# Moving ScalarE's request for a filter piece's rows from the end of an odd expert pair to the middle of the next even pair

## The chip, the cores and the metric

One NeuronCore of a Trainium2 chip runs the whole program. The metric is the device time of one execution in microseconds, lower is better. Times of the kernel before are the median of three runs; the trace is of one further, profiled execution.

## What is computed

One step of a two-layer network over 384 tokens of width 1024 (128 context tokens, 256 latent tokens). Layer 0 mixes tokens by attention, layer 1 by a long convolution whose filters are themselves computed. After each mixer comes a mixture of experts. The parts that matter here are the experts and the filters:

```python
# experts: 32, two chosen per token, hidden width 256
a = einsum('nd,edh->neh', t, w_gate); b = einsum('nd,edh->neh', t, w_up)
act = silu(a) * b * combine[:, :, None]
out = einsum('neh,ehd->nd', act, w_down)
# filters of layer 1: they depend on no token
filt = hdn @ w3 + b3
filt = filt * exp(-t_norm * exp(log_decay))
norm = sum(abs(filt), ...)          # and the spectrum of filt by a DFT
```

Everything is float32.

## The kernel before, in words

The experts are worked off in 16 **pairs** (q = 0 to 15), the same loop in both layers. A pair has up to 64 token rows per expert. TensorE multiplies the gathered tokens with the gate and up weights (line 903, 32 matmuls), ScalarE takes the silu out of the accumulator (line 1311), VectorE multiplies with the up half (line 1768), TensorE turns the result (line 909) and multiplies it with the down weights (line 917, 16 matmuls); ScalarE and VectorE copy one half each of the output (lines 1321 and 1785), and GpSimd scatters it to memory. In the midst of pair q TensorE also turns the gathered tokens of pair q + 1 (line 886) and ScalarE copies half of them out (line 1287, `gathered`). SyncE requests the weights: those of gate and up when line 903 of two pairs earlier is done (line 422), those of down likewise after line 917 (line 427). One pair's weights are 6 MB, in two ring slots.

A pair with more rows than fit has an **extra round**, which stands ahead of the pair proper: `extra(q)`, a conditional on every engine. There TensorE turns eight blocks (line 933), ScalarE and VectorE copy four each (lines 1297 and 1732), and TensorE's line 903 waits for both copies. In layer 0 pairs 6 and 7 have such a round in the trace.

The filters of layer 1 are computed in eight **pieces** (f = 0 to 7) inside layer 0's expert loop, in time that the engines have left. One piece takes three pairs:

- `load_filter` requests six transfers: two halves of the decay rows (line 414, 128 KB each, broadcast over all partitions), and for each half the rows of `w3` (line 416, 64 KB) and of `b3` (line 417, 1 KB). Its two waits are for TensorE's third tap matmul and ScalarE's decays of the piece before, since the tiles `eld` and `w3c` are single.
- `decay(f)` on ScalarE at the end of even pair 2f waits for both decay rows, then takes one exponential in place (line 1157), three more (line 1164), with a table load ahead (line 1157), and one back to silu (line 1166).
- In odd pair 2f + 1 TensorE makes the taps (line 608), VectorE multiplies them with the decays (line 1455), and ScalarE takes their absolute values (`sizes`, line 1170) at the pair's end.
- In even pair 2f + 2 TensorE makes the spectra (lines 625 to 630) and the sizes (line 639), ScalarE and VectorE copy them (lines 1176 and 1470), and ScalarE requests their store (`store_spectra`, line 1182, 768 KB) behind the next `decay`.

Each engine works its instructions off in the order of the program. On ScalarE that order holds for its transfer requests too: a request stands behind the waits ahead of it, and what follows a request waits until it is issued. The first piece is requested by SyncE, the other seven by ScalarE.

Of the kernel before, what the change touches and what calls it, by code (L numbers as in the profile page):

```python
# [149 lines left out]
def build(nc, a):  # L150

    ctx = ExitStack()
    with ctx:
# [5 lines left out]
        def sem(name):  # L159
            if name not in sems:  # L160
                sems[name] = ctx.enter_context(nc.semaphore(name))
            return sems[name]
# [141 lines left out]
        def turn_bank(q, half):  # L304
            return bank[half + (6 if q == 0 else 0)]
# [101 lines left out]
        def load_filter(sp, f):  # L407
            if f >= 1:
                sp.wait_ge(sem("taps_mm"), 3 * f)
                sp.wait_ge(sem("dec_set"), 4 * f)  # L410
            o, n = FILT[f]
            for d in range(2):
                lo = (2 * o + d) * D + n * FC
                sp.dma_start(eld[:, d * FC:(d + 1) * FC], a["hy_log_decay"][0, lo:lo + FC].partition_broadcast(P))\
                    .then_inc(sem("decay_in"), 16)
                sp.dma_start(w3c[0:FH, d * FC:(d + 1) * FC], a["hy_filt_w3"][0, :, lo:lo + FC]).then_inc(sem("w3_in"), 16)
                sp.dma_start(w3c[FH:FH + 1, d * FC:(d + 1) * FC], a["hy_filt_b3"][:, lo:lo + FC]).then_inc(sem("w3_in"), 16)
# [48 lines left out]
        def apart(eng):  # L466

            eng.sem_inc(sem("passed"), 1)
# [663 lines left out]
        def _(act):  # L1132
# [35 lines left out]
            def sizes(f):  # L1168
                act.wait_ge(sem("taps_done"), 3 * (f + 1))
                fn(dec.rearrange("p t d c -> p (t d c)"), hfb.rearrange("p t d c -> p (t d c)"), ACT.Abs).then_inc(sem("abs_done"), 1)  # L1170

            def spectra(f):
                act.wait_ge(sem("cf_mm"), 3 * f + 1)
                if f >= 1:
                    act.wait_ge(sem("cf_out"), 16 * f)
                fn(cfb[:, 0:2, :].rearrange("p b c -> p (b c)"), bank[6][:, :], ACT.Copy).then_inc(sem("cfa_set"), 1)
# [7 lines left out]
            def squares(n, x_set, base=0, step=2):  # L1184

                fn(idle[:, :], eps_col[:, :], ACT.Sqrt)
                for k in range(KD):
                    act.wait_ge(sem(x_set), base + step * (k + 1))
                    if n == 0 and k >= 2:
                        act.wait_ge(sem("sq_mm"), k - 1)  # L1190
                    if n % 2 == 1 and k == 0:
                        act.wait_ge(sem("xn_set"), KD * n)
                    if n >= 1 and k >= 3:
                        act.wait_ge(sem("acc_done"), (KD - 2) * (n - 1) + k - 2)
                    dst = sum_of(n) if n >= 1 and k == 0 else sq[:, k % 2, :]
                    fn(dst, xT[:, k, :], ACT.Square).then_inc(sem("sq_done"), 1)
                    if n == 4:
                        fn(hT[:, k, :], xT[:, k, :], ACT.Identity, scale=pc[:, R_FIN + k:R_FIN + k + 1],
                           bias=zero_col[:, 0:1]).then_inc(sem("h_act"), 1)
                act.wait_ge(sem("sq_mm"), SQ_BASE[n + 1])  # L1200
                if n == 4:
                    fn(rcol[:, :], bank[3][:, 0:TC], ACT.Sqrt, scale=1.0 / D, bias=eps_col[:, 0:1]).then_inc(sem("rt_done"), 1)
                    return
                fn(rstd[:, :], bank[3][:, 0:T], ACT.Sqrt, scale=1.0 / D, bias=eps_col[:, 0:1]).then_inc(sem("rt_done"), 1)

            def modulate(n, l, which):

                for k in range(H_ACT):
                    act.wait_ge(sem("xn_set"), KD * n + k + 1)
                    for c, (lo, hi) in enumerate(SPANS):  # L1210
                        fn(hT[:, k, lo:hi], hT[:, k, lo:hi], ACT.Identity, scale=amul[:, l, which, k, c:c + 1],
                           bias=ada[:, l, 3 * which, k, c:c + 1]).then_inc(sem("h_act"), 1)
# [51 lines left out]
            def moe(l, n_norm):  # L1264
                S_, B_ = sem, lambda name: l * PER_LAYER[name]
                squares(n_norm, f"mix{l}_done")
                modulate(n_norm, l, 1)

                act.wait_ge(S_("router_mm"), B_("router_mm") + 1)
                fn(lgT, bank[0][0:NG + NE, 0:T], ACT.Copy).then_inc(S_("lgt_set"), 1)  # L1270

                for g in range(2 * TC):
                    c, hf = divmod(g, 2)
                    act.wait_ge(S_("htok_mm"), B_("htok_mm") + g + 1)
                    dst = hTok[:, c, :].rearrange("p (k a) -> p a k", k=8)[:, 64 * hf:64 * (hf + 1), :]
                    fn(dst, bank[4 + g % 2].rearrange("p (a k) -> p a k", k=8), ACT.Copy).then_inc(S_("htok_set"), 1)

                act.wait_ge(S_("router_sub"), B_("router_sub") + 1)
                fn(gx.rearrange("p a b -> p (a b)"), gx.rearrange("p a b -> p (a b)"), ACT.Exp).then_inc(S_("gexp"), 1)
                act.wait_ge(S_("router_sub"), B_("router_sub") + 2)  # L1280
                fn(ev.rearrange("p a b -> p (a b)"), ev.rearrange("p a b -> p (a b)"), ACT.Exp).then_inc(S_("gexp"), 1)

                def gathered(q):
                    act.wait_ge(S_("gt_mm"), B_("gt_mm") + 2 * q + 1)
                    if q >= 1:
                        act.wait_ge(S_("gu_mm"), B_("gu_mm") + q)
                    fn(GT[:, 0:4], bank[0].rearrange("p (k s) -> p k s", k=4), ACT.Copy).then_inc(S_("gta_set"), 1)

                def extra(q):
                    lo = act.value_load(cumx[0:1, q:q + 1], min_val=0, max_val=2 * PAIRS)  # L1290
                    hi = act.value_load(cumx[0:1, q + 1:q + 2], min_val=0, max_val=2 * PAIRS)
                    with act.If(hi > lo):
                        act.wait_ge(S_("xnext"), l * PAIRS + q + 1)
                        apart(act)
                        with act.Fori(lo, hi) as x:
                            act.wait_ge(S_("xgt_mm"), x + 1)
                            fn(GTx[:, 0:4], turn_bank(q, 0).rearrange("p (k s) -> p k s", k=4), ACT.Copy).then_inc(S_("xgt_set"), 1)
                            act.wait_ge(S_("xgu_mm"), x + 1)
                            fn(S, bank[2][:, 0:EH], ACT.Silu).then_inc(S_("xsilu"), 1)
                            act.wait_ge(S_("xdn_mm"), 2 * (x + 1))  # L1300
                            act.wait_ge(S_("xslots"), x + 1)
                            fn(Yx[:, 0:HALF], bank[4][:, :], ACT.Copy).then_inc(S_("xy_set"), 1)

                gathered(0)
                act.wait_ge(S_("cum_set"), B_("cum_set") + 1)
                for q in range(PAIRS):
                    s = q % 2
                    if q >= 1:
                        extra(q)
                    act.wait_ge(S_("gu_mm"), B_("gu_mm") + q + 1)  # L1310
                    fn(S, bank[2][:, 0:EH], ACT.Silu).then_inc(S_("silu"), 1)  # L1311
                    if q + 1 < PAIRS:
                        gathered(q + 1)
                    if l == 0 and q % 2 == 0 and q >= 2:
                        spectra(q // 2 - 1)
                    if l == 0 and q == PAIRS - 1:
                        sizes(q // 2)
                    act.wait_ge(S_("dn_mm"), B_("dn_mm") + 2 * q + 1)
                    if q >= 2:
                        act.wait_ge(S_(f"scat{s}_"), B_(f"scat{s}_") + 16 * (q // 2))  # L1320
                    fn(Y[:, s, 0:HALF], bank[4][:, :], ACT.Copy).then_inc(S_("y_set"), 1)  # L1321
                    if q == 0:
                        apart(act)
                        extra(q)
                        apart(act)
                    if l == 0 and q % 2 == 0:
                        decay(q // 2)
                        if q >= 2:
                            store_spectra(q // 2 - 1)
                    if l == 0 and q % 2 == 1 and q < PAIRS - 1:  # L1330
                        load_filter(act, q // 2 + 1)
                        sizes(q // 2)

            moe(0, 1)

            squares(2, "moe_add")
# [740 lines left out]
```

## Time and profile before

| | |
|---|---|
| median of three runs | 1223.28 us (1220.71 to 1224.23) |
| profiled execution | 1220.09 us, of which 1218.1 us span |
| TensorE matmul busy | 1078.8 us, 89% of the span |
| ScalarE busy | 262.5 us, 22% |
| VectorE busy | 468.4 us, 38% |
| GpSimd busy | 186.1 us, 15% |
| bytes by transfers | 330.45 MB, mean 271 GB/s |
| mean granted clock of TensorE | 0.969 of full speed |

The span counts from the first to the last instruction; 2.0 us of the profiled execution lie around it. A line of the trace names an engine, a line of the program and the tiles; "idle before" is how long that engine stood still and what ended it. ACTq and SPq are the transfer requests of ScalarE and SyncE.

### The profile page before, as it was taken

What the parts mean: (1) busy time and instruction counts of PE and PEld (TensorE: products, weight loads), DVE (VectorE), ACT (ScalarE), POOL (GpSimd) and SP (SyncE); (2) the same over time, 40 slices, a digit from 0 to 9 for tenths busy, and PEclk for the clock granted to TensorE, in tenths of its full rate; (3) what the DMA queues carried; (4) which work ended last, traced back from release to release, by engine and by line L of the source; (5) the groups of instructions that cost most, each with busy time, mean ns of one, the idle gap of its engine ahead of it and who ended that gap; (6) DMA issues with size and microseconds to landing.
All of it is one profiled execution on the core that took longest, in us unless ns stands there. A gap on an engine that the chain in (4) does not pass through costs nothing.

```text
span 1218.1 us, 14747 instructions
## 1 busy us (share of the span) xinstructions
PE 1078.8 (89%) x5455; PEld 556.5 (46%) x5455; DVE 468.4 (38%) x1038; ACT 262.5 (22%) x514; POOL 186.1 (15%) x213
## 2 busy tenths in 40 slices
PE   5699978898999789999989999979989867888786
PEld 3344645554444244434355565638945322222224
DVE  2455667326122212323283336776371111111115
ACT  2211244214333121333331111000141011100014
POOL 1020000011322024221100001221013132111210
PEclk9999999999999999999999999999999989988989
DMA  9997895616699966999946110413190699999984
GB/s 356 395 337 286 247 342 215 277 56 251 224 399 407 375 254 252 413 407 406 383 169 233 46 59 0 177 65 142 67 362 21 260 413 411 414 414 408 412 344 156
DMA packets 95584, 330.45 MB, mean 271 GB/s; under 512 B 17546, under 2 KB 33322, under 8 KB 78724
## 3 DMA queue, kind: packets, MB, share of 16 engines
q1 hardware_dynamic: 68772, 300.72, 63.4%
q0 software_dynamic: 16848, 19.29, 4.7%
q10 hardware_dynamic: 9872, 9.21, 2.2%
q8 instruction: 58, 0.95, 0.3%
q14 instruction: 34, 0.28, 0.1%
HBM read 333.22 MB, written 35.35 MB: 303 GB/s over the span
## 4 chain that ended last, share of the span: by engine, by line
PE 65%; DMA 20%; DVE 7%; issue 3%; ACT 2%; SPq 2%; POOL 1%; ACTq 0%; POOLq 0%; DVEq 0%
PE bank L903 15%; DMA ring<-in_moe_w_up 12%; PE bank L1071 10%; PE bank L917 6%; PE bank L716 3%; PE bank L1113 3%; PE bank L832 3%; DMA ring<-in_w_ada 3%; PE bank L590 3%; PE bank L625 3%; PE bank L1102 2%; PE bank L1057 2%; PE bank L608 2%; DMA work<-token_vectors,curx 2%; DMA work<-token_vectors,work 1%
## 5 line engine op out<-in xcount | busy, mean ns | idle before, releaser
L903 PE MATMUL bank<-ring,work 128*64 128x512 f32 x1120 | 266.2, 631 | 42.7 <-DMA ring<-in_moe_w_up 28.8
L903 PEld LDWEIGHTS bank<-ring,work 128*64 128x64 f32 x1120 | 83.6, 145 | 214.4 <-issue 164.5
L917 PE MATMUL bank<-ring,work 128*64 128x512 f32 x560 | 129.1, 603 | 3.7 <-DVE work L1738 1.5
L1071 PE MATMUL bank<-hT,ring 128*128 128x384 f32 x384 | 126.3, 488 | 0.0
L1768 DVE SCALAR_TENSOR_TENSOR work<-bank,work 128x256 f32<-128x256 f32 x32 | 15.5, 484 | 253.3 <-ACT work L1311 234.3
L1071 PEld LDWEIGHTS bank<-hT,ring 128*128 128x128 f32 x384 | 72.2, 190 | 52.0 <-issue 2.3
L917 PEld LDWEIGHTS bank<-ring,work 128*64 128x64 f32 x560 | 37.4, 138 | 74.0 <-issue 64.0
L1785 DVE COPY work<-bank 128x512 f32<-128x512 f32 x32 | 22.1, 690 | 117.2 <-PE bank L917 101.6
L1311 ACT ACTIVATE work<-bank 128x256 f32<-128x256 f32 x32 | 12.3, 383 | 222.6 <-PE bank L903 221.9
L590 PE MATMUL bank<-ring,condS 128*32 128x256 f32 x768 | 47.4, 400 | 10.2 <-DVE ada L1432 5.5
L1937 POOL DMA_INDIRECT work<-token_vectors,work x28 | 28.7, 1024 | 154.9 <-PE bank L886 149.1
L1321 ACT ACTIVATE work<-bank 128x512 f32<-128x512 f32 x32 | 19.1, 596 | 121.6 <-PE bank L917 104.6
L1113 PE MATMUL bank<-work,ring 128*128 128x128 f32 (+1 forms) x256 | 42.2, 327 | 1.7 <-DVE work L1883 1.7
L1356 ACT ACTIVATE work<-bank,pc 128x128 f32<-128x128 f32 (+1 forms) x48 | 17.6, 418 | 119.9 <-PE bank L1071 119.9
L716 PE MATMUL bank<-hT,ring 128*64 128x384 f32 x256 | 43.0, 489 | 0.0
L886 PE MATMUL bank<-const,work 128*128 128x128 f32 x224 | 36.1, 285 | 7.5 <-DMA work<-token_vectors,work 7.5
L832 PE MATMUL bank<-work,ring 128*128 128x384 f32 x128 | 41.5, 487 | 0.7 <-DVE work L1590 0.7
L1942 POOL DMA_INDIRECT expert_rows<-work x30 | 30.1, 1003 | 77.7 <-DVE work L1785 74.4
L1113 PEld LDWEIGHTS bank<-work,ring 128*128 128x128 f32 x256 | 38.4, 190 | 5.5 <-issue 2.1
L1918 POOL MEMSET work<- 128x2048 f32 x2 | 3.6, 1804 | 240.4 <-DVE xT L1512 184.0
L1851 DVE TENSOR_SCALAR work<-work,pc 128x385 f32<-128x385 f32 x24 | 11.5, 480 | 74.2 <-ACT work L1356 74.2
L590 PEld LDWEIGHTS bank<-ring,condS 128*32 128x32 f32 x768 | 24.4, 114 | 33.0 <-DVE ada L1432 9.0
(306 smaller groups left out, 1488.7 us busy)
## 6 DMA issues: line engine op xcount, KB each, us to landing
ring<-in_moe_w_gate SPq DMA_DIRECT2D x32, 2048.0 KB, 17.5
ring<-in_moe_w_up SPq DMA_DIRECT2D x32, 2048.0 KB, 23.3
ring<-in_moe_w_down SPq DMA_DIRECT2D x32, 2048.0 KB, 23.2
ring<-in_w_ada SPq DMA_DIRECT2D x24, 2048.0 KB, 12.6
ring<-in_hy_w_in SPq DMA_DIRECT2D x6, 2048.0 KB, 15.4
expert_rows<-work POOLq DMA_DIRECT2D x6, 1024.0 KB, 15.2
filter_spectra<-work ACTq DMA_DIRECT2D x8, 768.0 KB, 17.5
work<-expert_rows SPq DMA_DIRECT2D x16, 384.0 KB, 6.8
```

The lines of the kernel that those rows point to most:

```text
L590: last = mm(ada_bank(t)[32 * j:32 * j + 32, 0:256], condS[:, 4 * hk + k, :], w[:, k, 256 * j:256 * j + 256], start=(hk == 0 and k == 0), s ...
L608: mm(bank[6 + c % 2][:, :], hd1[0:FH + 1, 1, c * P:(c + 1) * P], w3c, start=True, stop=True)\
L625: last = mm(dst, m[:, off:off + P], smd_of(f)[:, part if part < 2 else r, c, :], start=(j == 0), stop=(j == len(ops) - 1))
L716: last = mm(bank[m % 2][b * HD:(b + 1) * HD, 0:T], wq[:, k, h * HD:(h + 1) * HD], hT[:, k, :], start=(k == 0), stop=(k == KD - 1))
L832: last = mm(bank[m % 2][:, 0:T], wo[:, k, m * P:(m + 1) * P], oT[:, k, :], start=(k == 0), stop=(k == KD - 1))
L886: last = tr(bank[half][:, kk * P:(kk + 1) * P], G[:, q % 2, k * P:(k + 1) * P], ident)
L903: last = mm(bank[2][WIN * j:WIN * (j + 1), :], gt[:, k, WIN * j:WIN * (j + 1)], gu[:, :, j, k, :], start=(k == 0), stop=(k == KD - 1))
L917: last = mm(bank[b + hf][WIN * j:WIN * (j + 1), :], AT[:, k, WIN * j:WIN * (j + 1)], dn[:, j, k, hf * HALF:(hf + 1) * HALF], start=(k == 0 ...
L1071: last = mm(bank[n % 2][:, 0:T], w[:, k, (n % 4) * P:(n % 4 + 1) * P], hT[:, k, :], start=(k == 0), stop=(k == KD - 1))
L1113: last = mm(bank[4 + m % 2][:, lo:hi], wout[:, k, m * P:(m + 1) * P], st[:, 2, k, a0:a1], start=(k == 0), stop=(k == KD - 1))
L1937: ind(out=G[:, q % 2, :], out_offset=None, in_=hD, in_offset=at_rows(tab[:, 4 * q + 1:4 * q + 2]), bounds_check=T - 1, oob_is_err=False).t ...
L1942: ind(out=yD, out_offset=at_rows(tab[:, 4 * q:4 * q + 1]), in_=Y[:, q % 2, :], in_offset=None, bounds_check=2 * T - 1, oob_is_err=False).t ...
```

## The change

The request for the rows of piece f, f = 1 to 7, moves from the end of odd pair 2f − 1 on ScalarE into even pair 2f, behind the silu and the copy of the next pair's gathered tokens and ahead of the copy of the spectra. Nothing else is changed; the same transfers are made, with the same waits.

```diff
                     if q + 1 < PAIRS:
                         gathered(q + 1)
                     if l == 0 and q % 2 == 0 and q >= 2:
+                        load_filter(act, q // 2)
                         spectra(q // 2 - 1)
                     if l == 0 and q == PAIRS - 1:
                         sizes(q // 2)
@@
                         if q >= 2:
                             store_spectra(q // 2 - 1)
                     if l == 0 and q % 2 == 1 and q < PAIRS - 1:
-                        load_filter(act, q // 2 + 1)
                         sizes(q // 2)
```

## Rows read from the trace of the kernel before

**Rows 1.** Busy time by stretch; columns explained by the first line.

```profile
core 0: us, PE busy (x) PEld busy (x) DVE busy (x) ACT busy (x) POOL busy (x), PEclk, DMA share, GB/s
340.00:400.00 60.00, 59.84 (x284) 26.59 (x282) 16.27 (x27) 20.40 (x29) 15.77 (x17) 1.00 1.02 403
400.00:470.00 70.00, 58.43 (x270) 23.96 (x268) 13.56 (x24) 13.73 (x21) 12.67 (x16) 0.98 0.69 263
470.00:610.00 140.00, 136.11 (x624) 57.38 (x620) 43.94 (x76) 45.17 (x63) 35.47 (x38) 1.00 1.02 400
```

**Rows 2.** TensorE's waits from 300 to 610 us: total, times, longest.

```profile
PE bank L903 <- ACT work L1297: 6.1, 2, 4.5
PE bank L903 <- DMA ring<-in_moe_w_up: 0.5, 1, 0.5
```

**Rows 3.** The chain that ended last, in order of time: start, length, what.

```profile
319.68 8.74 PE bank L903 x32
...
408.27 8.81 PE bank L903 x32
...
438.90 1.28 ACT L1157
...
445.02 7.11 PE bank L903 x32
...
535.01 0.23 PE bank L909 x2
...
1069.52 9.31 PE bank L903 x32
```

**Rows 4.** Timeline of all engines: pair 1's line 903, then pair 6's extra round.

```profile
319.68 1.12 PE L903 MATMUL bank<-ring,work 128*64 128x512 f32 x2 [2.06 <-DVE work L1722]
...
402.93 0.35 ACTq L414 DMA_DIRECT2D hT<-in_hy_log_decay  x1
402.93 0.69 DVE L1455 TENSOR_TENSOR work<-bank,work 128x512 f32<-128x512 f32 x1 [0.35 <-PE bank L608]
405.74 0.68 DVE L1732 COPY work<-bank 128x512 f32<-128x512 f32 x1
405.96 1.48 ACT L1170 ACTIVATE work<-work 128x1536 f32<-128x1536 f32 x1 [5.20 <-issue]
407.62 0.60 ACT L1297 ACTIVATE work<-bank 128x512 f32<-128x512 f32 x1 [0.18 <-issue]
```

**Rows 5.** Timeline of ScalarE in pair 6, up to the extra round of pair 7.

```profile
431.57 0.60 ACT L1287 ACTIVATE work<-bank 128x512 f32<-128x512 f32 x1 [0.20 <-PE bank L886]
444.37 0.60 ACT L1297 ACTIVATE work<-bank 128x512 f32<-128x512 f32 x1
```

**Rows 6.** Timeline of all engines, pairs 9 to 11, a pair of pairs without extra rounds.

```profile
507.14 0.35 ACTq L414 DMA_DIRECT2D hT<-in_hy_log_decay  x1
508.77 0.36 ACTq L414 DMA_DIRECT2D hT<-in_hy_log_decay  x1
510.24 0.47 ACTq L417 DMA_DIRECT2D sq<-in_hy_filt_b  x1
514.17 0.38 ACT L1311 ACTIVATE work<-bank 128x256 f32<-128x256 f32 x1 [1.93 <-PE bank L903]
514.74 0.60 ACT L1287 ACTIVATE work<-bank 128x512 f32<-128x512 f32 x1 [0.19 <-PE bank L886]
521.45 0.60 ACT L1321 ACTIVATE work<-bank 128x512 f32<-128x512 f32 x1 [4.38 <-PE bank L917]
522.07 1.28 ACT L1157 ACT_TABLE_LOAD   x1
525.52 0.57 ACTq L1182 DMA_DIRECT2D filter_spectra<-work  x1
527.28 0.20 ACT L1166 ACTIVATE idle<-eps_col 128x1 f32<-128x1 f32 x1
532.75 0.38 ACT L1311 ACTIVATE work<-bank 128x256 f32<-128x256 f32 x1 [5.27 <-PE bank L903]
533.17 0.49 DVE L1768 SCALAR_TENSOR_TENSOR work<-bank,work 128x256 f32<-128x256 f32 x1 [7.73 <-ACT work L1311]
```

**Rows 7.** Request to landing of decay rows (line 414): pieces 4, 3, all by ScalarE, SyncE's second.

```profile
DMA to landing us min/median/max: 9.9/9.9/9.9
...
DMA to landing us min/median/max: 10.3/10.3/10.3
...
DMA to landing us min/median/max: 7.0/9.5/12.8
...
DMA to landing us min/median/max: 4.0/4.0/4.0
```

**Rows 8.** Request to landing of the spectra's stores (line 1182), 350 to 600 us.

```profile
DMA to landing us min/median/max: 11.3/17.7/19.5
```

**Rows 9.** TensorE's granted clock (PEclk) around its idle times; columns as in rows 1.

```profile
405.00:408.40 3.40, 0.13 (x2) 0.13 (x4) 1.42 (x3) 2.08 (x2) 0.00 (x0) 1.00 1.04 421
408.40:411.80 3.40, 3.40 (x10) 0.95 (x12) 0.00 (x0) 0.00 (x0) 0.00 (x0) 0.50 1.03 381
445.90:449.30 3.40, 3.40 (x18) 1.15 (x16) 0.00 (x0) 0.00 (x0) 0.00 (x0) 1.00 1.04 384
```

## The prediction

> **What bounds the kernel now.** I read the busy time by stretch first. The change lies in layer 0's expert loop, some 300 to 610 us. TensorE is busy there for 59.84 of 60 us and for 136.11 of 140 us at full clock; only from 400 to 470 us does it stand still for more than 11 us [rows 1]. The transfers are full in the same stretches (share 1.02, 400 to 403 GB/s) and not between 400 and 470 us, 263 GB/s. Both engines of the bound run side by side: TensorE waited for weights once, 0.5 us [rows 2]. ScalarE works a third of the time, so a move on it costs only where somebody waits for it. TensorE's waits name that place: line 903 waited twice for ScalarE's copy in the extra round (line 1297), 6.1 us together, 4.5 us the longer [rows 2]. These are the rounds of pair 6 (TensorE resumes at 408.27 us) and pair 7 (445.02 us) [rows 3]; 4.5 us belong to the first and 1.6 us to the second. Both lie behind the code that is changed: the round of pair 6 stands behind the end of odd pair 5, from which the request goes, and the round of pair 7 behind the end of even pair 6, where `decay(3)` waits for the rows that are now asked for later. Everywhere else ScalarE's next silu is what can be late.
>
> **What goes, at the end of odd pairs.** Six requests take from 507.14 to 510.71 us, 3.6 us, and hold back the absolute values behind them [rows 6]. In an ordinary pair ScalarE waits for TensorE after that anyway (the silu at 514.17 us had an idle 1.93 us before it [rows 6]), so nothing is won in six of the seven. In the extra round of pair 6 it is won: the requests began at 402.93 us, the absolute values ran from 405.96 to 407.44 us and the copy from 407.62 us [rows 4]. VectorE had finished the last tap at 402.93 + 0.69 = 403.62 us. Without the requests the absolute values end at about 405.1 us and ScalarE's copy at about 405.95 us. Next late is VectorE's half of the same copy, which ended at 405.74 + 0.68 = 406.42 us [rows 4]. So TensorE starts at 406.45 us and not at 408.27 us: **−1.8 us**. Its idle time falls from 4.5 to 2.7 us. After the 4.5 us it was granted half its clock (0.50, the 1.2 GHz level) for 3.4 us, which made the 32 matmuls 8.81 us long; after 1.6 us of idle time the clock stayed at 1.00 and they took 7.11 us [rows 3, 9]. The nearest row is TensorE's idle 2.06 us before pair 1's line 903 [rows 4], whose 32 matmuls then took 8.74 us [rows 3]: the clock fell there too. The bounds are 0 and −1.7 us, and I take 0.
>
> **What comes, in even pairs.** The requests stand behind the copy of line 1287, which began at 514.74 us [rows 6]. A request need not wait for the end of a computation ahead of it: the store of 525.52 us was issued amid the exponentials that stand ahead of it. I put the first request 0.1 to 0.6 us behind that copy's start and the second decay row 1.6 us after the first (508.77 − 507.14), together 2.0 us behind the copy's start. ScalarE's spectra copy is pushed back by some 2.5 us, to end near 519.5 us; the output copy behind it started only at 521.45 us [rows 6], and TensorE asks for that spectra copy only after line 917, so this costs nothing; without the cover it would cost at most its own 2.5 us per pair.
>
> `decay` waits for both rows. Landing took 7.0 to 12.8 us over all fourteen; of the seven second rows the quickest took 9.9 us (piece 4), that of piece 3 10.3 us [rows 7], and the others up to 12.8 us. The decay started 522.07 − 514.74 = 7.3 us behind the copy's start. With a landing of L it now starts 2.0 + L behind it, **L − 5.3 us later**: 4.6 to 7.5 us with the rows' L. The table load is no cover, for it follows the wait of its activation.
>
> *Extra round of pair 7.* In pair 6 the copy of line 1287 began at 431.57 us, the decay's table load at 438.90 us and the extra round's copy at 444.37 us, right behind the decay [rows 3, 5]. TensorE waits for it already, so the whole delay is on the path. For L I take 10.3 us, the same piece's at its old place: **+5.0 us** (4.6 to 7.5 by the second rows; −1.3, cut to 0, by SyncE's 4.0 us [rows 7], when few transfers ran). TensorE's idle time becomes 1.6 + 5.0 = 6.6 us, longer than the 4.5 us after which the clock fell, so line 903 behind it starts at half clock: 8.81 − 7.11 = 1.7 us up to 9.31 − 7.11 = 2.2 us, the latter from layer 1, [rows 3]; I take **+1.8 us**. Neither is absorbed, because the transfers run dry in this stretch [rows 1] and SyncE's next requests follow line 903, so they shift along.
>
> The Trainium skill (DMA: Bandwidth & Descriptors, "Anatomy of one DMA — SWDGE (gpsimd) path") gives a transfer as about 2.0 us plus its bytes over 436 GB/s, an estimate of some 2.3 us for a row of 128 KB on a different request path. By it the rows would be there before the decay wants them and the sum would lose its +5.0 and +1.8 us; the trace disagrees with 7.0 us for the quickest of fourteen.
>
> *Silus of odd pairs.* Decay, with store and the way back to silu, took 527.48 − 522.07 = 5.4 us; the next silu came at 532.75 us, 18.0 us behind the copy's start [rows 6]. Now ScalarE is free at 2.0 + L + 5.4, late by L − 10.6 us. Then VectorE's product ends at 533.66 us and TensorE wants it at 535.01 us [rows 3, 6], 1.35 us more. So a pair pays L − 11.95 us where that is above 0: at most 0.9 us, for the slowest row of 12.8 us. Bounds for six pairs are 0 and about 2 us, if each row takes as long as at its old place; most of them lie under the limit, so I take **+0.5 us**.
>
> Sum: −1.8 + 5.0 + 1.8 + 0.5 = **+5.5 us** on the profiled 1220.09 us, hence 1225.6 us. That execution was 3.2 us under the median of the runs, so the median becomes 1223.28 + 5.5 = **1228.8 us**.
>
> **Rivals.**
>
> *A softer extra round.* At 431 us the transfers have just started again, so L could be 8 us: then the decay is 2.7 us late, the gap 4.3 us; and pair 6's round may also keep its clock. −1.8 − 1.7 + 2.7 + 1.7 = +0.9 us, 1224.2 us. For it: 263 GB/s in this stretch. Against it: 4 MB of weights are requested just ahead of the rows.
>
> *The row is there in time.* The other side: ScalarE's row lands before the decay wants it, and only what the odd pair's end lost is seen. Place: the decay of pair 6; price: −1.8 us, −3.5 us with the clock kept, so 1221.5 to 1219.8 us; it decides at L = 5.3 us. For it: SyncE's 4.0 us. Against it: all fourteen of ScalarE's, 7.0 us and up. The Trainium skill's formula, above, would give this result.
>
> *Rows behind the store.* A later decay makes a later store, on the same queue as the rows. The store was issued 3.45 us behind the decay's start and took 11.3 to 19.5 us [rows 6, 8]. Issued 5 to 7 us later, at up to 532.5 us, it ends by 552.0 us, while the next even pair's rows, 33.4 us on, are asked for from 548.5 us. If the rows queue behind it, L grows by up to 3.5 us, the silus of five ordinary odd pairs are late by some 1.5 us and the extra round by 2 us: +5.5 + 7.5 + 2 = +15 us, 1238 us at most, 1235 us at half of it. Against it: the median store, 17.7 us, is out by 550.2 us, about when the second row is requested.
>
> *It does not do what it says.* If ScalarE's requests went out no later than now, nothing would change, 1223 us. The program's order excludes that; no chance of its own.
>
> **Chances.** Forecast 0.55, soft round 0.25, row in time 0.08, behind the store 0.12. A measurement of this kernel tells about 0.3% (3.7 us) from no change. Slower by more: most of the forecast's cases and the store's, 0.63; faster by more only at the outer end of the row-in-time case, 0.04; within it 0.33. The range runs from inside the soft round, 1223.0 us, to the store's case at half its price, 1235.0 us.
>
> **What would show it.** In the trace after: requests of line 414 in even pairs, some 0.1 to 0.6 us behind the start of line 1287; idle time before `decay`'s table load, put down to the decay rows, about 5 us; TensorE's wait for line 1297 in pair 6's round down from 4.5 to 2.7 us, in pair 7's up from 1.6 to 6.6 us, with a clock of 0.50 behind it; silus of odd pairs close behind ScalarE's return. Wrong if the second rows land in under 8 us in mid-pair, if TensorE waits for silus or output copies in many pairs, or if the shift of layer 0 is taken back by a wait for weights later.

## The result and the profile after

The changed kernel took 1231.59 us, median of six runs (1227.60 to 1235.37), the kernel before 1222.87 us in six beside it: 1.0059 times as long, 95% interval 1.0039 to 1.0080, or 7.2 us more. This ratio, here and below, is estimated over all runs; it is not the quotient of the two medians, which lie 8.7 us apart. The profiled execution took 1231.95 us with a span of 1230.0 us, 11.9 us over the one before.

Not all of the 11.9 us come from the change. In executions of kernels that are the same up to there, the first line 903 starts anywhere from 300.8 us (before) to 305.3 us (after); 4.5 us of the difference between the two profiles lie ahead of everything that was edited. I therefore compare stretches inside the loop, from the start of pair 2's line 903:

| us | before | after | difference |
|---|---|---|---|
| pair 2 to pair 6's extra round | 72.2 | 70.4 | −1.8 |
| that round to pair 6 proper | 15.6 | 13.9 | −1.7 |
| pair 6 to pair 7's extra round | 21.2 | 28.5 | +7.3 |
| that round to pair 7 proper | 13.9 | 15.8 | +1.9 |
| pair 7 to pair 15 | 134.05 | 134.73 | +0.7 |

The first four lines sum to +5.8 us (122.8 to 128.6 us), with the fifth +6.5 us; from pair 15 to the end of the program the two differ by 1.0 us more. The fifth line is TensorE's wait for weights ahead of pair 14, 1.23 us here and 0.54 us before.

Busy time by stretch, kernel after, columns as in rows 1. TensorE is nearly full outside 400 to 480 us, and in that stretch its mean clock is 0.94:

```profile
core 0: us, PE busy (x) PEld busy (x) DVE busy (x) ACT busy (x) POOL busy (x), PEclk, DMA share, GB/s
300.00:400.00 100.00, 96.54 (x480) 45.61 (x479) 29.58 (x58) 30.35 (x43) 33.01 (x37) 0.98 0.81 314
400.00:480.00 80.00, 64.69 (x285) 27.40 (x286) 16.13 (x28) 14.23 (x22) 13.50 (x17) 0.94 0.65 250
480.00:620.00 140.00, 137.41 (x618) 57.82 (x616) 48.08 (x74) 43.04 (x61) 34.98 (x37) 0.98 1.03 399
```

TensorE's waits from 300 to 625 us, kernel after. ScalarE's copy, 6.1 us in rows 2, is no releaser any more. In its place stand GpSimd's sums (line 2006), once, and VectorE's copy (line 1732):

```profile
PE bank L639 <- POOL hT L2006: 5.6, 1, 5.6
PE bank L903 <- DVE work L1732: 3.5, 2, 2.7
...
PE bank L903 <- DMA ring<-in_moe_w_up: 1.2, 1, 1.2
...
PE bank L933 <- DMA work<-token_vectors,curx: 0.6, 1, 0.6
```

Timeline of ScalarE in pair 6, kernel after, to be set against rows 5. The requests go out 0.06 us behind the start of the copy (line 1287); that of the second decay row follows 1.7 us later. The table load runs at once; the first exponential then stands idle for 6.0 us until the rows are there:

```profile
432.47 0.60 ACT L1287 ACTIVATE work<-bank 128x512 f32<-128x512 f32 x1 [0.20 <-PE bank L886]
432.53 0.37 ACTq L414 DMA_DIRECT2D hT<-in_hy_log_decay  x1
434.19 0.36 ACTq L414 DMA_DIRECT2D hT<-in_hy_log_decay  x1
439.80 1.28 ACT L1157 ACT_TABLE_LOAD   x1
447.11 0.63 ACT L1157 ACTIVATE hT<-hT 128x512 f32<-128x512 f32 x1 [6.04 <-DMA hT<-in_hy_log_decay]
448.04 0.72 ACT L1164 ACTIVATE work<-hT,const 128x512 f32<-128x512 f32 x1 [0.29 <-POOL hT L2006]
452.51 0.60 ACT L1297 ACTIVATE work<-bank 128x512 f32<-128x512 f32 x1 [1.02 <-PE bank L933]
```

The last line is the surprise: ScalarE was back from its decay at 451.5 us and still waited 1.0 us, for TensorE's turn of the gathered tokens (line 933). TensorE had been held up elsewhere. Timelines of GpSimd and of TensorE in the same stretch, kernel after:

```profile
425.24 0.99 POOL L1952 DMA_INDIRECT expert_rows<-work,curx  x1 [20.97 <-DVE work L1741]
430.61 0.19 POOL L1957 COPY curx<-work 128x4 int32 x1 [4.37 <-DMA expert_rows<-work,curx]
431.67 1.04 POOL L1960 DMA_INDIRECT work<-token_vectors,curx  x1 [0.88 <-POOL curx L1957]
442.02 0.19 POOL L1968 COPY curx<-work 128x4 int32<-128x4 int32 x1 [9.31 <-DMA work<-token_vectors,curx]
442.98 1.03 POOL L1970 DMA_INDIRECT work<-token_vectors,curx  x1 [0.77 <-POOL curx L1968]
445.33 1.81 POOL L2004 TENSOR_TENSOR hT<-work 128x768 f32<-128x768 f32 x1
447.22 0.73 POOL L2006 TENSOR_TENSOR hT<-hT 128x256 f32<-128x256 f32 x1
```

```profile
410.84 7.09 PE L903 MATMUL bank<-ring,work 128*64 128x512 f32 x32 [2.71 <-DVE work L1732]
448.00 1.87 PE L639 MATMUL bank<-const,hT 128*128 128x1 f32 x8 [5.56 <-POOL hT L2006]
450.51 1.97 PE L933 MATMUL bank<-const,work 128*128 128x128 f32 x8 [0.64 <-DMA work<-token_vectors,curx]
453.26 9.01 PE L903 MATMUL bank<-ring,work 128*64 128x512 f32 x32 [0.78 <-DVE work L1732]
```

GpSimd's part of an extra round is a chain of transfers, each waited for before the next: the scatter of the round's output (line 1952), the gather of a possible further window (line 1960), the gather for the next pair's round (line 1970). Only then come its scatter and its sums of filter sizes (lines 2004 and 2006), for which TensorE waits in line 639. The gather of line 1960 held GpSimd from 431.67 to 442.0 us. In the kernel before the same chain ran like this:

```profile
429.80 1.04 POOL L1960 DMA_INDIRECT work<-token_vectors,curx  x1 [0.88 <-POOL curx L1957]
...
430.98 0.37 SPq L422 DMA_DIRECT2D ring<-in_moe_w_gate  x1
...
432.25 0.19 POOL L1968 COPY curx<-work 128x4 int32<-128x4 int32 x1 [1.41 <-DMA work<-token_vectors,curx]
437.45 0.73 POOL L2006 TENSOR_TENSOR hT<-hT 128x256 f32<-128x256 f32 x1
```

There the gather was out 1.2 us ahead of SyncE's request for 4 MB of weights (430.98 us), and back 2.4 us after its start. In the kernel after it was issued at 431.67 us and the weights at 431.88 us, as this line of SyncE's timeline shows:

```profile
431.88 0.37 SPq L422 DMA_DIRECT2D ring<-in_moe_w_gate  x1
```

Why the order became so close shows one step earlier. The scatter and the weights' request both follow TensorE, and both came 3.5 us earlier against pair 2. But the scatter (line 1952) now held GpSimd up for 5.4 us (425.24 to 430.61 us) and not for 4.4 us. Pair 7's weights, whose last request SyncE had made at 401.88 us before and at 406.25 us after, did not come earlier with the round: the scatter began 22.5 us behind that request before and 19.0 us after. The transfers were busier in the 4 us behind its start, with a DMA share of 0.37 and not 0.17 (columns as in rows 1; before, then after):

```profile
424.40:428.40 4.00, 4.00 (x22) 1.64 (x20) 0.00 (x0) 0.00 (x0) 0.96 (x1) 1.00 0.17 62
...
425.20:429.20 4.00, 4.00 (x22) 1.67 (x20) 0.00 (x0) 0.00 (x0) 0.99 (x1) 1.00 0.37 138
```

So two things hold up pair 7's round: decay rows that come late, and gathers that are overtaken by weights. The chain of what ended last goes through the gathers (10.05 us and 7.04 us of it in pair 6); ScalarE's rows are second latest, 1 us behind. Of the +7.3 us from pair 6 to pair 7's round, 6.0 us are ScalarE's idle time for the rows; the other 1.3 us come from GpSimd's chain, 0.3 us as ScalarE's wait for the sums (ahead of its second exponential, line 1164) and 1.0 us as its wait for TensorE. Which of them is a cause by itself, the profile alone can't say.

### The profile page after: what moved, and what is told of

Read it like the earlier page. It is cut to its first block, busy times and chain, and to the rows that moved or that the text cites. A ratio compares the mean times of both kernels' runs of the same rounds, so it can differ in the third digit from the quotient of the medians.

```text
span 1230.0 us, 14747 instructions
## 1 busy us (share of the span) xinstructions
PE 1085.1 (88%) x5455; PEld 561.0 (46%) x5455; DVE 477.8 (39%) x1038; ACT 262.3 (21%) x514; POOL 187.0 (15%) x213
## 4 chain that ended last, share of the span: by engine, by line
PE 64%; DMA 22%; DVE 6%; issue 3%; ACT 2%; SPq 2%; POOL 1%; POOLq 0%; DVEq 0%; ACTq 0%
PE bank L903 14%; DMA ring<-in_moe_w_up 12%; PE bank L1071 10%; PE bank L917 6%; PE bank L716 3%; PE bank L1113 3%; PE bank L832 3%; DMA ring<-in_w_ada 3%; PE bank L590 3%; DMA work<-token_vectors,curx 3%; PE bank L625 2%; PE bank L1102 2%; PE bank L1057 2%; PE bank L608 2%; DMA expert_rows<-work,curx 1%
## 5 line engine op out<-in xcount | busy, mean ns | idle before, releaser
L1071 PEld LDWEIGHTS bank<-hT,ring 128*128 128x128 f32 x384 | 72.2, 190 | 52.0 <-issue 2.3
L590 PE MATMUL bank<-ring,condS 128*32 128x256 f32 x768 | 48.0, 404 | 11.9 <-DMA ring<-in_w_ada 6.4
```

The costliest lines, as they stand in the source:

```text
L590: last = mm(ada_bank(t)[32 * j:32 * j + 32, 0:256], condS[:, 4 * hk + k, :], w[:, k, 256 * j:256 * j + 256], start=(hk == 0 and k == 0), s ...
L1071: last = mm(bank[n % 2][:, 0:T], w[:, k, (n % 4) * P:(n % 4 + 1) * P], hT[:, k, :], start=(k == 0), stop=(k == KD - 1))
```

## The experiments

Timed against before beside them; "stretch" is from pair 2's to pair 7's line 903 in the profiled execution (before 122.8 us, after 128.6 us), the number on which mechanisms are told apart. "Piece 3 behind" is short for piece 3's request behind the round.

| kernel | ratio (95%) | stretch | round of pair 6: wait, 32 matmuls | pair 6 to round of pair 7 |
|---|---|---|---|---|
| before | | 122.8 | 4.5, 8.8 | 21.2 |
| after | 1.0059 (1.0039 to 1.0080) | 128.6 | 2.7, 7.1 | 28.5 |
| piece 3 alone | 1.0050 (1.0031 to 1.0069) | 131.4 | 3.1, 7.1 | 29.7 |
| all but piece 3 | 1.0009 (0.9998 to 1.0020) | 122.8 | 4.5, 8.8 | 21.2 |
| change and filler | 1.0065 (1.0043 to 1.0088) | 131.6 | 4.1, 8.8 | 28.3 |
| behind the round | 1.0020 (0.9992 to 1.0049) | 123.6 | 3.1, 9.8 | 21.6 |
| piece 3 behind the round | 1.0023 (1.0003 to 1.0044) | 128.3 | 2.7, 7.1 | 27.9 |
| change, weights wait | 0.9965 (0.9945 to 0.9984) | 121.8 | 3.1, 7.1 | 21.6 |
| behind the round, weights wait | 0.9984 (0.9963 to 1.0005) | 122.7 | 2.7, 9.9 | 21.6 |
| before, weights wait | 0.9974 (0.9953 to 0.9995) | 122.8 | 4.5, 8.8 | 21.2 |
| piece 3 behind, weights wait | 0.9986 (0.9966 to 1.0006) | 121.4 | 2.7, 7.1 | 21.6 |
| behind the round, sums first | 1.0016 (0.9993 to 1.0039) | 123.0 | 4.3, 8.8 | 21.6 |

TensorE's wait of 3.1 us ahead of pair 6's round, in three of these profiles, is one for weights. In these three the loop was already 1.5 to 1.8 us ahead at pair 2 (33.5 to 33.8 us from pair 0 to pair 2, 35.3 us before), because pair 1's matmuls had kept their clock. Their stretches therefore hold some waiting for weights that the others don't have.

### Where the cost lies: piece 3 alone, all but piece 3

```diff
                     if l == 0 and q % 2 == 0 and q >= 2:
-                        load_filter(act, q // 2)
+                        if q == 6:
+                            load_filter(act, q // 2)
...
                     if l == 0 and q % 2 == 1 and q < PAIRS - 1:
+                        if q != 5:
+                            load_filter(act, q // 2 + 1)
                         sizes(q // 2)
```

This is the first kernel's diff against after; the second has `q != 6` and `q == 5` in the two conditions.

> Only the request of piece 3 moves, from the end of pair 5 into pair 6; the other six stay at the ends of their odd pairs. If the cost of the change lies between the extra rounds of pairs 6 and 7 (rows of piece 3 late, or GpSimd's transfers late, each in that stretch), this kernel takes all of it: 5 to 10 us over before, ratio 1.004 to 1.008. If late silus of the ordinary odd pairs make the cost (the rival), it is close to before, within 2 us.

> The other half: six requests move, that of piece 3 stays. If the cost lies between the extra rounds, nothing is left of it: within 2 us of before, TensorE's waits in ordinary pairs unchanged, although the decays of six pieces start 3 to 7 us later. If late silus or stores make the cost, it is 5 us or more over before.

Piece 3's request alone gives the whole cost, 1.0050; the six others give none, 1.0009 with 1 in the interval and the stretch as before. ScalarE's waits in the kernel with the six others show that their rows come just as late, without harm: 21.7 us in six decays, while no silu of an odd pair was waited for.

```profile
ACT hT L1157 <- DMA hT<-in_hy_log_decay: 21.7, 6, 5.2
```

So late silus, and rows delayed behind stores, do not make the cost.

### The rows alone: change and filler

```diff
                     if l == 0 and q % 2 == 1 and q < PAIRS - 1:
+                        act.wait_ge(sem("taps_mm"), 3 * (q // 2 + 1))
+                        for n in range(12):
+                            fn(filler[:, n:n + 1], eps_col[:, :], ACT.Silu).then_inc(sem("cond_set"), 1)
+                            act.wait_ge(sem("cond_set"), 2 + 12 * (q // 2) + n + 1)
                         sizes(q // 2)
```

The diff is against after; the silus write a small tile of their own, `filler`.

> The change, and at the end of each odd pair twelve chained one-element silus on ScalarE that take about the 3 us which the six requests took there, so pair 6's round starts no earlier than before. Theory of the gathers: GpSimd's chain is again ahead of the request of weights, its sums are no wait; what is left is the rows' lateness alone. Theory of the rows: 5 to 6 us of delay plus 1.7 us of half clock, with nothing won ahead, 6 to 9 us over before. If the gathers alone made the cost, it is within 2 us of before.

Measured 1.0065, by the ratio 8.0 us over before. Twelve silus took 2.8 us; TensorE's wait in pair 6's round was 4.1 us again and its clock fell as before. GpSimd's gather was issued at 430.47 us, 1.5 us ahead of the weights, and held it up for 1.4 us only. What remains is the rows, TensorE's timeline:

```profile
444.20 1.09 PE L934 MATMUL bank<-const,work 128*128 128x128 f32 x8 [0.66 <-DMA work<-token_vectors,curx]
453.21 9.14 PE L904 MATMUL bank<-ring,work 128*64 128x512 f32 x32 [7.92 <-ACT work L1298]
```

(Lines are one higher here: 904 is 903.) The turn was done at 445.3 us and line 903 waited 7.9 us for ScalarE, whose decay had stood idle 7.35 us for its rows. So late rows alone make the whole loss. In the stretch it is larger than the change's (131.6 and 128.6 us), since most of the −3.5 us ahead of the rows is missing.

### The gathers alone: requests behind the round, for all pieces and for piece 3

```diff
                     if q >= 1:
                         extra(q)
+                    if l == 0 and q % 2 == 0 and q >= 2:
+                        load_filter(act, q // 2)
                     act.wait_ge(S_("gu_mm"), B_("gu_mm") + q + 1)
...
                     if l == 0 and q % 2 == 1 and q < PAIRS - 1:
-                        load_filter(act, q // 2 + 1)
                         sizes(q // 2)
```

The diff is against before. The second kernel is the one before with `q == 6` in this condition and no request at the end of pair 5.

> All seven requests stand at the top of the even pair, behind the extra round and ahead of the wait for the silu: out of the way of the copy in pair 6's round, as in the change, yet 7 to 8 us earlier than there, so the rows of piece 3 land long before the decay wants them. Theory of the rows: the cost goes, the gain stays, 3.4 us under before (1.8 us of the copy, 1.6 us of the clock). Theory of the gathers: GpSimd's chain of small transfers in pair 6 is overtaken by SyncE's request of weights because pair 6's round ends earlier; then TensorE still waits some 5 us for GpSimd's sums (line 2006 to line 639) and for the next gather, and the kernel is 0 to 5 us over before.

> Only piece 3's request moves, and only behind pair 6's extra round, ahead of the silu: the edit of the kernel with piece 3 alone, with its rows asked for 6 us earlier. Rows are in time, so this shows the gathers by themselves wherever pair 6's round starts early and keeps its clock. If they alone can make the wait: in the profile, where 32 matmuls of pair 6's round take 7.1 us, GpSimd's second gather lands 8 us late and TensorE waits 5 us for the sums; the times spread over 1219 to 1229 us. If the gathers only suffer when the rows are late too: no such wait, and 3 us under before throughout.

With all pieces the times fell into two groups, three at 1220.1 to 1221.9 us and seven at 1226.2 to 1231.1 us. The profile is of the first group, and none was taken of the second. It caught an execution in which pair 6's round gained little: its weights landed late (a wait of 3.1 us) and the clock fell, 9.8 us for 32 matmuls. GpSimd's gather went out 0.8 us ahead of the weights and nothing was late. That run could not tell the theories apart. The kernel with piece 3 alone behind the round could, and its profile shows the gathers at work with the rows in time:

```profile
431.24 0.19 POOL L1960 COPY curx<-work 128x4 int32 x1 [6.04 <-DMA expert_rows<-work,curx]
432.31 1.05 POOL L1963 DMA_INDIRECT work<-token_vectors,curx  x1 [0.88 <-POOL curx L1960]
438.74 1.28 ACT L1157 ACT_TABLE_LOAD   x1
440.03 0.63 ACT L1157 ACTIVATE hT<-hT 128x512 f32<-128x512 f32 x1
440.15 0.19 POOL L1971 COPY curx<-work 128x4 int32<-128x4 int32 x1 [6.80 <-DMA work<-token_vectors,curx]
446.13 1.86 PE L639 MATMUL bank<-const,hT 128*128 128x1 f32 x8 [4.75 <-POOL hT L2009]
446.17 0.72 ACT L1164 ACTIVATE work<-hT,const 128x512 f32<-128x512 f32 x1 [5.51 <-POOL hT L2009]
```

The first exponential has no idle time, so the rows were there. The scatter had held GpSimd up for 7.0 us (424.20 to 431.24 us) this time. The gather (line 1963 here) was issued at 432.31 us, behind the weights' 430.82 us, and left GpSimd idle for 6.8 us; TensorE waited 4.75 us for the sums. ScalarE's second exponential waited for them too, 5.51 us; it must not write the decays before the sums have read them. The stretch is 128.3 us, close to the change's 128.6 us. So the gathers alone can make the loss too. They don't always make all of it: this profile is of the slowest of twelve executions (1230.37 us), the others reach down to 1221.19 us, and the ratio, 1.0023, is less than half of the change's loss.

Over all twelve profiles the scatter held GpSimd up for 5.4 to 7.0 us in the five in which pair 6's round kept its clock (7.1 us), and for 3.9 to 4.7 us in the seven others. In the three of the five in which SyncE does not wait, the gather went out from 0.2 us ahead of the weights to 1.5 us behind them; in the five others without that wait it went out 0.8 to 1.6 us ahead.

### Both away: the weights wait

```diff
                     sp.wait_ge(S_("gu_mm"), B_("gu_mm") + q - 1)
+                    if l == 0 and q == 8:
+                        sp.wait_ge(S_("xnext_in"), 16 * 8)
                 load_gu(sp, l, q)
```

SyncE asks for pair 8's gate and up weights only when GpSimd's gather for pair 7's round has landed. This edit was put on the change, on the kernel with all requests behind the round, on the kernel with piece 3's behind it, and on before.

> The change, and SyncE's request of pair 8's gate and up weights also waits until GpSimd's gather for pair 7's extra round has landed, so that this one request can no longer overtake GpSimd's three serial transfers. By the first four runs two causes are there: late decay rows (6 to 8 us of wait in pair 7's round, alone in the kernel with the filler) and the overtaken gathers (5 to 6 us of wait, at the same place and time, so they don't add up). Expected: GpSimd's sums are no wait any more, the rows remain: 3 to 7 us over before, TensorE waits some 5 to 7 us for ScalarE's copy in pair 7's round. If the overtaken gathers are the whole cause: 3 us under before.

> The requests behind the extra round (rows in time), and the same wait of SyncE. Both causes are gone: no run near 1230 us, all runs in one group, 0 to 3.5 us under before (0 where TensorE's clock falls at pair 6's round or its weights land late, 3.5 us where neither does). If the slow runs of the kernel with the requests behind the round had another cause than the overtaken gathers, they stay, some six in ten at 1226 to 1231 us.

> The kernel before with SyncE's wait alone: a control for the cost of the wait itself, and whether before's few runs at 1230 us are the same race. The transfers stand still from 454 to 466 us anyway, so a request 5 us later costs nothing: within 1 us of before's usual runs, and none at 1228 us or more.

> The same with SyncE's wait ahead of pair 8's weights. Rows in time, gathers not overtaken, the six other requests at the ends of their pairs: 0 to 3.6 us under before, and no run above 1226 us. It should equal the change with that wait (ratio 0.9965) within 0.2%.

On the change I expected 3 to 7 us over before, because only the gathers were to be helped. That was wrong: it has the lowest ratio of all kernels, 0.9965 (1221.47 us, 1217.79 to 1224.77; before beside it 1223.90 us). The wait moved the weights' request from 0.65 us ahead of the first decay row's to 6.5 us behind the second one's, and so helped the rows as well. ScalarE's and SyncE's timelines, change with the wait:

```profile
431.31 0.36 ACTq L414 DMA_DIRECT2D hT<-in_hy_log_decay  x1
437.82 0.37 SPq L422 DMA_DIRECT2D ring<-in_moe_w_gate  x1
438.21 0.63 ACT L1159 ACTIVATE hT<-hT 128x512 f32<-128x512 f32 x1
```

The second row landed after this time, the first after 2.9 us:

```profile
DMA to landing us min/median/max: 3.3/3.3/3.3
```

The weights' request was all that was moved, and both delays went. Both causes thus have one root: 4 MB of weights asked for at the moment when small transfers are due on which the next round depends. On before the wait changes nothing in the stretch (122.8 us), which shows that it costs nothing by itself; its ratio is 0.9974, with an interval that ends at 0.9995. Of before's 34 executions beside it nine took 1228 us or more, up to 1232.33 us; of this kernel's twelve none did, and of the 36 of all three kernels with the wait in this comparison none. So the wait may remove late executions of before as well; no late execution of before was profiled, and the cause is not shown. The gain of the change with the wait must be read beside this control: its twelve runs are 1.7 us under the control's in the mean, hardly clear of the spread. What is shown is that the loss is gone. With piece 3's request behind the round the stretch is 121.4 us and the ratio 0.9986, 0.2% above that of the change with the wait, with the median nearly the same (1221.37 us). One run of 1228.12 us was not expected, and I don't explain it. With all requests behind the round and the wait, the profiled execution lost 2.4 us in pair 0 already, ahead of any edit, and the ratio, 0.9984, has 1 inside. As expected, the two groups that this kernel had without the wait became one, 1221.8 to 1226.5 us. Part of what is won at pair 6's round is given back at pair 7's: in both kernels with 7.1 us in the first, the 32 matmuls of the second take 8.8 us.

### Behind the round, sums first

```diff
                 for q in range(PAIRS):
+                    if l == 0 and q % 2 == 0 and q >= 2:
+                        size_sums(q // 2 - 1)
                     extra(q)
...
-                    if l == 0 and q % 2 == 0 and q >= 2:
-                        size_sums(q // 2 - 1)
```

The diff is against the kernel with all requests behind the round.

> The requests behind the extra round, and GpSimd makes the sizes' sums ahead of its part of the extra round instead of behind it. TensorE's wait of line 639 for these sums goes. Theory: the sums only showed the lateness of the whole chain, and the gather of pair 7's round, behind the same chain, is waited for instead (line 933): two groups of runs as before the edit. Rival: the place of the sums is the cause; then all runs are at 1220 to 1223 us.

On the sums' place it says nothing, since pair 6's round was not early and the gather went out ahead of the weights. All ten runs lay between 1224.84 and 1230.49 us, in one group, which neither theory gave. Why the round was not early stands in its VectorE timeline:

```profile
410.78 2.02 DVE L1464 TENSOR_TENSOR hT<-work 128x256 f32<-128x256 f32 x1
412.73 0.68 DVE L1733 COPY work<-bank 128x512 f32<-128x512 f32 x1
```

The addition of line 1464 took 0.42 us in the kernel before (there at 405.40 us, line 1463). Here GpSimd's first sum ran from 410.61 to 412.53 us, at the same time, and it took 2.02 us; VectorE's copy for the round started 1.6 us later for it, and TensorE waited 4.3 us and lost its clock. The moved sums had met VectorE's additions on the tiles of the same piece. That one engine slows the other is what the times suggest; no run was made for it. It explains the lost gain and no more: the stretch is 123.0 us, 0.2 us over before. The profiled execution lies 10.0 us over before elsewhere: 3.0 us ahead of the first line 903, 2.4 us in pair 0, where TensorE waits for VectorE's product, and 2.8 us from pair 7 to pair 15, where a wait for weights ahead of pair 14 (1.7 us) was followed by 8.7 us for the 32 matmuls; the rest comes behind pair 15. Why all ten runs are slow stays open.

## Why the prediction was right, and where only by luck

The forecast was +5.5 us for the median, 1228.8 us; measured were +7.2 us by the ratio and a median of 1231.6 us, inside the range. In the stretch itself it is +5.8 us. That this is so close is luck: the clock came out 1.7 us better than forecast, the delay of pair 7's round 2.3 us worse, and the wait that ended last there was not the one that was forecast. By its own steps:

- **What the odd pairs' end gives** was right to a tenth: −1.8 us, with VectorE's half of the copy next late (a wait of 2.71 us put down to line 1732, forecast 2.7 us).
- **The clock at pair 6's round** was the wrong end of its range: 0 taken, −1.7 us measured. The clock stayed at full speed after 2.7 us of idle time here; over the four profiles with that wait it did so in three and fell in one (9.9 us for the 32 matmuls), so the term is a draw between its two ends and not a fixed value. The row on which the caution rested is such a draw too: ahead of pair 1's line 903 TensorE stood idle for 2.1 us in all twelve profiles, and the 32 matmuls took 7.1 us in four of them and 8.7 to 8.8 us in eight.
- **The extra round of pair 7** was forecast at +5.0 and +1.8 us and came at +7.3 and +1.9 us. The term that was mis-sized is L. The second row of piece 3 took about 12.9 us (434.19 to 447.1 us) and not the 10.3 us of its old place; with the filler 14.2 us. It was asked for 2.3 us behind 4 MB of weights. Against that stood an error the other way: I had put the table load behind the wait, and it runs ahead of it, which hides 1.3 us. With the request 0.3 us earlier than assumed, this gives 6.0 us of idle time.
- **The sign that did not come.** I forecast that TensorE's wait for ScalarE's copy (line 1297) would grow from 1.6 to 6.6 us. In the trace after it is not there: TensorE waited 5.6 us for GpSimd's sums, 0.6 us for the gather and 0.8 us for VectorE's half of the copy. The late rows are a sufficient cause, as the kernel with the filler shows (7.9 us of wait for line 1297), but here the gathers ended 1 us later.
- **What the step left out** is GpSimd. I counted the six requests and the queue they stand in, but not what an earlier start of pair 6's round does to others. SyncE's request and GpSimd's scatter both came 3.5 us earlier against pair 2. But pair 7's weights did not, so the scatter ran beside more of them and took 5.4 instead of 4.4 us. The gather's lead over the next weights fell from 1.2 to 0.2 us, and GpSimd's idle time behind it grew by 8 us. The times and the DMA shares suggest this reason for the longer scatter; no run separates it. In the change this wait and that for the rows lie over each other, so the sum hardly shows it; with the rows in time it takes the gain of 3.5 us and another 5.5 us (stretch 128.3 us). My text even held that the transfers run dry in this stretch, which is true of its mean and false of the moment in which the gather was due.
- **Silus of odd pairs**: +0.5 us forecast, 0 measured. Rows of ordinary pairs made the decay wait 2.8 to 5.8 us, and the silu behind it was late once, by 0.4 us, for which TensorE did not wait.
- **The rivals**: a softer round did not come, though its half on pair 6's clock did. The row in time needed an emptier queue: in the change with the waiting weights the row took 3.3 us. The estimate of 2.3 us from the Trainium skill (DMA: Bandwidth & Descriptors, "Anatomy of one DMA — SWDGE (gpsimd) path") is not far from that. Rows behind the store did not show: from the second row's request to the first exponential it was 9.7 to 12.9 us in all seven pieces, about what the rows took before. One idle time of ScalarE's is put down to the store (2.6 us, line 1176), but it is as long as those of the other pieces, in which the requests are issued (2.5 to 2.7 us).

The 1.7 us between forecast and measured ratio can't be placed: from pair 7 to the end the profile after has 1.7 us more, of which 0.7 us are a wait for weights, and the ratio's own interval is 2.5 us to either side.

## What to carry to other kernels

A request that is moved changes two things: when its data come, and when everything starts that it stood ahead of. Follow the second as far as the first. Where a serial chain of small transfers and a request for megabytes are due within a microsecond or two of each other, write their order down with a wait: here one wait on SyncE, in a stretch where the transfers had slack, turned a loss of 0.6% into a ratio of 0.9965, which is no loss and, beside the control's 0.9974, at most a small gain. And look in the profile for a short transfer that was short only because it went out just ahead of a large one; its duration is no property of it.

## What the runs showed of the hardware

- A gather that GpSimd waits for took 2.2 us when issued 1.2 us ahead of SyncE's 4 MB, and held GpSimd up from 431.67 to 442.0 us when issued 0.2 us ahead of them. A decay row of 128 KB took 3.3 us with no weights asked for and 12.9 to 14.2 us behind them, on another engine's queue. The Trainium skill (DMA: Bandwidth & Descriptors, "Issuing engines are not separate DMA queues") says that transfers from all engines run on the same 16 DMA engines and interleave; the traces agree as far as they show it: small transfers of two engines were slowed by a third engine's large one, by a factor of about four.
- VectorE's addition of 128 × 256 elements took 2.02 us beside an addition of GpSimd's and 0.42 us without one.
- ScalarE's table load ran ahead of the wait of its first exponential (439.80 us against 447.11 us), where another table load, ahead of the first silu of the loop, began only after the wait (before: 307.95 us, 10.09 us of idle time ahead of it).
- TensorE's clock after an idle time: after 2.1 us, ahead of pair 1, full in four profiles and fallen in eight (the 32 matmuls 7.1 and 8.7 to 8.8 us); after 2.7 us full in three profiles and at half in one (the 32 matmuls 7.1 and 9.9 us); after 3.1 us, of a wait for weights, full in two and at half in one (7.1 and 9.8 us). After 5.6 us in pair 6 it was at half, 0.50 (1.2 GHz) from 448 to 451 us:

```profile
448.00:451.00 3.00, 2.36 (x11) 2.28 (x12) 0.00 (x0) 2.95 (x4) 1.03 (x1) 0.50 1.03 404
```
